# Input norm on per-token values, first input units in memory of their own, and a final stage in column halves, in a fused hybrid layer

## The chip, the cores and the metric

One core of a Trainium2 chip runs the whole program as one launch. The metric is the device time in microseconds of that core. All arrays are float32; matrix products are made of a high and a low part of each operand (fp32r), in three products each.

## What is computed

One inference step with one layer, for 512 latent tokens and 128 context tokens (640 in all), D = 2048:

```python
sh1, sc1, g1, sh2, sc2, g2 = split(silu(cond) @ w_ada + b_ada)      # for latent and for context tokens
h = rmsnorm(x, n1g) * (1 + sc1) + sh1
glu_in, q, k, v, ga, gb = split(h @ w_in)
conv_out = conformer_conv(glu_in)            # width 31, LayerNorm, swish, pointwise to 2048
attn_out = attention(rope(q), rope(k), v, cached k, cached v, sink)
x = x + g1 * ((sigmoid(ga) * conv_out + sigmoid(gb) * attn_out) @ w_out)
h2 = rmsnorm(x, n2g) * (1 + sc2) + sh2
gate, idx = top_k(softmax(h2 @ w_router).T, capacity)                # 16 experts: 64 latent, 16 context slots each
x = x + g2 * scatter_add(idx, gate * ((silu(h2[idx] @ w_g) * (h2[idx] @ w_u)) @ w_d))
y = rmsnorm(x, final_g)                      # outputs: y for both groups, k and v of the context
```

## The kernel before, in words

Each engine has a program of its own, written in order; they meet at semaphores. Weights come in units of 128 x 2048 values (1 MB), loaded by SyncE's queue in exactly the order of their use. Until the experts begin, the units go through a ring of four slots, `raw` (`raw_use` gives slot and count of use, L74). A slot is given back by `raw_freed`, two per use.

**Start.** SyncE's queue (`sync_program`, L328) loads `cond`, `x` in four parts (1.25 MB each), two units of `w_ada`, then units 0 and 1 of `w_in` into slots 2 and 3, then 30 more units of `w_ada`, each behind its slot. ScalarE squares the 16 channel tiles of `x` (L926) and VectorE adds them up (L1265). TensorE spreads the mean over all partitions with a matrix of 1/D (`mean_over_channels`, L625). VectorE adds EPS and takes the reciprocal (L1268, L1269), ScalarE the root (L939), VectorE makes one Newton step (L1271 to L1274), all on 128 x 640 values, and then the low halves of the two input units (`split_lo`, L1237); their high halves are ScalarE's (`split_hi`, L908).

A pair of ada units (shift and scale of one channel tile) is used by `ada_unit` (L589), 16 small matmuls of two passes per unit. The row is copied out (L915), folded (L597) and gets its bias (L1256). Then VectorE modulates the tile of `x` (L1280 to L1287), ScalarE and VectorE make its high and low half (L931, L1290), and TensorE uses it at once for both input units (`first_units`, L640; matmuls L610 to L612). So the first two dense units are made tile by tile beside the stream of ada units. When they end, ScalarE copies v of unit 0 out of PSUM (L962), makes the high half of unit 2, and TensorE goes on with unit 2 when both halves are there (`dense_start`, L617).

**Middle.** Dense units 2 to 39, then 32 gate units with attention, the convolution and two ada units to each, then attention out, conv out and `w_out` (16 units, 192 to 207 in the ring). In the last stage tokens and their modulated form go to DRAM (`tokens_acc`, `tokens_z`).

**Experts.** The expert weights are 24 units per expert through a ring of twelve (`ering`), which lies over the activations and raw slots 0 and 1. Unit j is loaded to slot (j + 10) % 12: units 0 and 1 go to the two raw slots when these are free, unit 2 when the last dense unit is done, and from unit 12 on each waits for the low half of the unit twelve before it (`ex_lo`, L371). After the routing (top-k on VectorE) POOL gathers the 80 token rows of expert 0 with an indirect DMA (L546) and gathers each next expert's rows beside the current one. TensorE needs the gathered rows to start. ScalarE casts a unit to its high half (L1160), VectorE subtracts for the low half (L1668), TensorE multiplies (L875). An expert's output columns 0 to 1023 are complete at unit 19, columns 1024 to 2047 at unit 23 (`slots_y`, L1689); POOL adds them to `tokens_acc` with one indirect DMA (`scatter`, L550).

**Tail.** When the last scatter has landed, SyncE's queue loads five tiles of 128 tokens (L381, 1 MB each). ScalarE squares each with its sum (L1197), VectorE and ScalarE make 1/rms for all five at once (L1738 to L1744, root L1200). Per tile VectorE scales (L1755), TensorE transposes in four groups (L899), ScalarE (L1205) and VectorE (L1749) multiply two groups each with the norm's weights, and SyncE's queue writes two outputs of 512 KB (L386). VectorE's order in that loop is: scale tile q, then its two groups of tile q - 1.

## Time and profile before

| | us |
|---|---|
| median of 3 runs | 3214.08 (3208.89 to 3214.21) |
| the profiled execution | 3212.56 |
| its span in the profile | 3210.8 |

The span is the time from the first to the last record of that one execution; the 1.8 us around it belong to the run. In the profile "busy" is time in which an engine executes, "idle before" what stood ahead of an instruction and what released it, and PEclk the share of its full clock that TensorE was granted (1.00 or 0.50). PEld is the loading of weights into TensorE, which lies beside matmuls. A DMA issue is named by the engine whose queue it stands in (SPq, POOL); its landing is when its semaphore is reached. "Issue" in the chain is time in which an engine waited for nothing that the profile shows.

### The profile page before, as it was taken

The numbers are of one execution on the slowest core, as the hardware profiler recorded it, in microseconds if no ns is written. First come the engines' busy times: TensorE is split into PE (matmuls) and PEld (weight loads), VectorE is DVE, ScalarE is ACT, GpSimd is POOL, SyncE is SP. The second block draws the span as 40 slices with busy tenths as digits, with TensorE's granted clock in tenths as the row PEclk, the third lists the DMA queues.
The fourth block names the chain that finished last, engine by engine and source line by source line (L and its number), as shares of the span: only waits on it lengthen the run. The fifth ranks groups of instructions, "written<-read, shape, count | busy, mean of one in ns | idle before, by whom it ended". The sixth has DMA issues, their size and how long they took to land.

```text
span 3210.8 us, 51984 instructions
## 1 busy us (share of the span) xinstructions
PE 3036.2 (95%) x20428; PEld 2579.3 (80%) x20428; DVE 1942.0 (60%) x2023; ACT 1349.6 (42%) x1479; POOL 275.8 (9%) x433
## 2 busy tenths in 40 slices
PE   5899999999999999989999999599999999999995
PEld 4899999989898998989999999366666666666663
DVE  6333322246565656665234333799999999998894
ACT  3211111133332333323112111477777777777774
POOL 0011110001111110110011111000000000000000
PEclk9999999999999999999999999799999999999997
DMA  9633332234444444453335432899999999999994
GB/s 367 266 128 119 119 127 78 78 112 171 171 168 180 165 167 173 174 211 114 128 148 187 130 128 85 309 364 398 382 379 369 389 387 389 384 378 374 382 376 139
DMA packets 124009, 746.06 MB, mean 232 GB/s; under 512 B 16720, under 2 KB 27008, under 8 KB 44080
## 3 DMA queue, kind: packets, MB, share of 16 engines
q1 hardware_dynamic: 97088, 636.54, 51.3%
q0 software_dynamic: 26768, 107.34, 10.8%
q8 instruction: 113, 1.85, 0.2%
q14 instruction: 40, 0.33, 0.0%
HBM read 681.60 MB, written 55.66 MB: 230 GB/s over the span
## 4 chain that ended last, share of the span: by engine, by line
PE 77%; DVE 9%; DMA 5%; issue 5%; ACT 3%; SPq 0%; DVEq 0%; POOL 0%; ACTq 0%; POOLq 0%
PE pu L875 22%; PE pu L610 15%; PE pu L611 15%; PE pu L612 15%; DVE elo L1668 4%; PE pt L589 2%; PE pt L721 2%; DMA raw<-in_w_ada 2%; ACT ehi L1160 2%; DVE xe L1680 1%; PE ps L691 1%; DVE wlo L1237 1%; PE ps L699 1%; PE pt L709 1%; DMA raw<-in_w_in 1%
## 5 line engine op out<-in xcount | busy, mean ns | idle before, releaser
L610 PE MATMUL pu<-hhi,whi 128*128 128x320 f32 x3328 | 1049.9, 315 | 19.9 <-DVE hlo L1446 11.0
L611 PE MATMUL pu<-hlo,whi 128*128 128x320 f32 x3328 | 1032.4, 310 | 0.0
L612 PE MATMUL pu<-hhi,wlo 128*128 128x320 f32 x3328 | 1032.3, 310 | 0.0
L1668 DVE TENSOR_TENSOR elo<-ering,ehi 128x2048 fp32r<-128x2048 f32 x384 | 874.8, 2288 | 107.0 <-ACT ehi L1160 103.3
L1160 ACT CAST ehi<-ering 128x2048 fp32r<-128x2048 f32 x384 | 731.4, 1912 | 238.2 <-PE pu L875 238.0
L610 PEld LDWEIGHTS pu<-hhi,whi 128*128 128x128 f32 x3328 | 629.3, 189 | 26.7 <-issue 17.5
L611 PEld LDWEIGHTS pu<-hlo,whi 128*128 128x128 f32 x3328 | 629.3, 189 | 1.9
L612 PEld LDWEIGHTS pu<-hhi,wlo 128*128 128x128 f32 x3328 | 628.6, 189 | 0.0
L908 ACT CAST whi<-raw 128x2048 fp32r<-128x2048 f32 x112 | 213.0, 1902 | 486.4 <-PE pu L612 463.0
L1237 DVE TENSOR_TENSOR wlo<-raw,whi 128x2048 fp32r<-128x2048 f32 x112 | 256.6, 2291 | 256.6 <-ACT whi L908 255.9
L875 PE MATMUL pu<-ehi,xhi 128*80 128x512 f32 x1024 | 322.0, 395 | 2.2
L875 PE MATMUL pu<-ehi,xlo 128*80 128x512 f32 x1024 | 320.4, 394 | 0.0
L875 PE MATMUL pu<-elo,xhi 128*80 128x512 f32 x1024 | 320.0, 393 | 0.0
L1408 DVE SCALAR_TENSOR_TENSOR ctmp<-zt,taps,ctmp 128x670 f32<-128x670 f32 x232 | 212.5, 916 | 28.3 <-DVE ctmp L1408 19.2
L875 PEld LDWEIGHTS pu<-ehi,xhi 128*80 128x80 f32 x1024 | 149.3, 148 | 89.8 <-DVE elo L1668 9.3
L875 PEld LDWEIGHTS pu<-elo,xhi 128*80 128x80 f32 x1024 | 151.6, 148 | 85.5 <-issue 0.7
L875 PEld LDWEIGHTS pu<-ehi,xlo 128*80 128x80 f32 x1024 | 151.5, 148 | 85.5 <-issue 0.7
L875 PE MATMUL pu<-ehi,hthi 128*80 128x512 f32 x512 | 162.8, 399 | 0.0
L875 PE MATMUL pu<-ehi,htlo 128*80 128x512 f32 x512 | 159.8, 393 | 0.0
L875 PE MATMUL pu<-elo,hthi 128*80 128x512 f32 x512 | 159.8, 393 | 0.0
L589 PE MATMUL pt<-raw,condw 128*32 128x128 f32 x3072 | 108.6, 286 | 16.8 <-DMA raw<-in_w_ada 16.7
L1023 ACT COPY pt_sb<-pt 128x512 f32<-128x512 f32 (+1 forms) x80 | 41.8, 523 | 183.3 <-PE pt L709 112.6
(252 smaller groups left out, 2619.3 us busy)
## 6 DMA issues: line engine op xcount, KB each, us to landing
ering<-in_w_experts SPq DMA_DIRECT2D x384, 1024.0 KB, 7.8
raw<-in_w_ada SPq DMA_DIRECT2D x96, 1024.0 KB, 7.0
raw<-in_w_in SPq DMA_DIRECT2D x72, 1024.0 KB, 4.8
raw<-in_w_attn_out SPq DMA_DIRECT2D x16, 1024.0 KB, 6.3
raw<-in_w_out SPq DMA_DIRECT2D x16, 1024.0 KB, 4.8
gates_tanh<-th POOLq DMA_DIRECT2D x32, 320.0 KB, 2.4
gl<-gates_tanh POOLq DMA_DIRECT2D x32, 320.0 KB, 3.5
raw<-in_w_conv_out SPq DMA_DIRECT2D x8, 1024.0 KB, 4.8
```

Source lines behind the costliest of these rows:

```text
L589: last = nc.tensor.matmul(bank[g:g + 32, 0:128], condw[:, kt, 30 - 2 * u:62 - 2 * u], raw[:, slot, kt * 128:kt * 128 + 128], start=u == 0 ...
L610: nc.tensor.matmul(o, whi[:, dk, w:w + 128], hi[:, kt, cols], start=kt == 0, stop=False)
L611: nc.tensor.matmul(o, whi[:, dk, w:w + 128], lo[:, kt, cols], start=False, stop=False)
L612: last = nc.tensor.matmul(o, wlo[:, dk, w:w + 128], hi[:, kt, cols], start=False, stop=kt == kts - 1)
L721: last = nc.tensor.matmul(pt[:, 0, 0:128], vg[:, v, :], pt_sb[:, 128 * b:128 * b + 128], start=b == 0, stop=b == len(vs) - 1)
L875: last = nc.tensor.matmul(pu[0:SLOTS, 2 * (h % 2) + c, :], left, ring[:, j % AHEAD, w:w + 512], start=k == 0 and left is hi and ring is eh ...
L908: nc.scalar.copy(whi[:, dk, :], raw[:, slot, :]).then_inc(hi_ready, 1)
L1023: last = nc.scalar.copy(pt_sb[:, 0:min(w, 512)], pt[:, 0, 0:min(w, 512)])
L1160: nc.scalar.copy(ehi[:, j % AHEAD, :], ering[:, slot, :]).then_inc(ex_hi, 1)
L1237: nc.vector.tensor_tensor(wlo[:, dk, :], raw[:, slot, :], whi[:, dk, :].bitcast(F32), ALU.subtract).then_inc(lo_ready, 1)
L1408: nc.vector.scalar_tensor_tensor(out=dst, in0=ztf[:, ds(zb, CO)], scalar=w, in1=ctmp[:, :], op0=ALU.mult, op1=ALU.add).then_inc(conv_done, 1)
L1668: nc.vector.tensor_tensor(elo[:, j % AHEAD, :], ering[:, slot, :], ehi[:, j % AHEAD, :].bitcast(F32), ALU.subtract).then_inc(ex_lo, 1)
```

## The change

Six things, with the code below:

- Input units 0 and 1 are loaded to `wfirst`, which lies over the end of `hlo`, ahead of all ada units, and the first four ada units are loaded without a wait. Every later position in the ring is two lower (`G_Q = A1 - 2`).
- The sums of squares are turned to one value per token and partition (five matmuls with one column each); the root and Newton step are made on 128 x 5 values; a product with the identity and a second `mean_over_channels` spread the result, which carries the factor D, over all partitions. TensorE does that after the first ada unit. The low half of unit 0 is made before the spread result is read, that of unit 1 after.
- Unit 1 of the first two dense units is made four channel tiles behind unit 0 (`LAG`), and its last five tiles follow the last of unit 0. ScalarE makes the high half of unit 2 before it copies v of unit 0.
- The load of expert unit 12 waits for the first gather.
- The last expert's scatter is two, one for each half of the columns. The tail's loads and squares are in halves too; the sums of both are added. Tile 0 has its 1/rms by itself, tiles 1 to 4 together (`FIN`). A root of one value ahead of the squares loads the table early.
- `rope_a`, `pool_passed` and `vec_passed`, on which nothing waits, are one semaphore. The hunks of that are left out below.

```diff
-G_Q = A1
+G_Q = A1 - 2
+LAG = 4
...
-    return raw_use(j if j < 2 else j + 2, 0, 1, 0, 0)
+    return raw_use(j, 0, 1, 0, 0)
...
+    wfirst, o = at("wfirst", [128, 2, UNIT], F32, R0 - 2 * UNIT * 4)
...
+        for d in range(2):
+            sp.dma_start(wfirst[:, d, :], a["w_in"][d]).then_inc(first_loaded[d], 16)
         for j in range(A1):
-            load(a["w_ada"][ada_of(j)], *ada_use(j), first=j < 2)
-            if j == 1:
-                for d in range(2):
-                    load(a["w_in"][d], 2 + d, 0, first=True)
+            load(a["w_ada"][ada_of(j)], *ada_use(j), first=j < RAW)
...
             if j < ERING - LEAD:
-                sp.wait_ge(raw_freed[j], 2 * (G_E // RAW))
+                sp.wait_ge(raw_freed[j], 2 * ((G_E + RAW - 1 - j) // RAW))
...
+            if j == ERING:
+                sp.wait_ge(xe_loaded, 16)
...
-        sp.wait_ge(ex_lo, NE * EU)
-        sp.wait_ge(y_added, 16 * NE)
-        for q in range(5):
-            sp.dma_start(fin[:, q, :], acc_d[128 * q:128 * q + 128, :]).then_inc(unit_loaded[q], 16)
+        sp.wait_ge(ex_lo, NE * EU - 5)
+        for h in range(2):
+            sp.wait_ge(y_last[h], 16)
+            cols = slice(1024 * h, 1024 * h + 1024)
+            for q in range(5):
+                sp.dma_start(fin[:, q, cols], acc_d[128 * q:128 * q + 128, cols]).then_inc(unit_loaded[5 * h + q], 16)
...
-            pool.wait_ge(y_made, 2 * e + 4)
-            scatter(e)
+            if e + 1 < NE:
+                pool.wait_ge(y_made, 2 * e + 4)
+                scatter(e)
+        for h in range(2):
+            pool.wait_ge(y_made, 2 * NE + 1 + h)
+            pool.indirect_dma_start(acc_d[:, :], bass.IndirectOffsetOnAxis(ap=idx_all[:, NE - 1:NE], axis=0),
+                                    ysl[:, 1024 * h:1024 * h + 1024], None, element_offset=1024 * h,
+                                    compute_op=ALU.add).then_inc(y_last[h], 16)
...
-        mean_over_channels(t1, ps, HALF, norm_mm)
+        for q in range(5):
+            last = nc.tensor.matmul(ps[:, 0, q:q + 1], t1[:, 128 * q:128 * q + 128], ones[:, 0:1], start=q == 0,
+                                    stop=True, skip_group_check=True)
+        last.then_inc(norm_mm, 1)
...
         def first_units(kt):
...
+            first_unit(0, kt)
+            if kt >= LAG:
+                first_unit(1, kt - LAG)
...
+            if j == 0:
+                pe.wait_ge(norm_t, 3)
+                mean_over_channels(t2, ps, HALF, norm_mm)
...
+        for kt in range(KT - LAG, KT):
+            first_unit(1, kt)
...
+        first_hi(0)
+        act.wait_ge(norm_t, 2)
+        nc.scalar.activation(nrm[:, 2, 0:5], nrm[:, 1, 0:5], ACT.Sqrt).then_inc(norm_sq, 1)
+        first_hi(1)
...
         for d in range(2 * NKV):
+            if d == 0:
+                split_hi(*raw_use(G_Q, 1, U, 0, 2), 2, 0)
             if d < NKV:
...
-            split_hi(*raw_use(G_Q, 1, U, 0, d + 2), d + 2, d % 2)
+            if d:
+                split_hi(*raw_use(G_Q, 1, U, 0, d + 2), d + 2, d % 2)
...
+        nc.scalar.activation(fst[:, 4, 7:8], ones[:, 0:1], ACT.Sqrt)
+        for h in range(2):
+            for q in range(5):
+                act.wait_ge(unit_loaded[5 * h + q], 32 * NE + 16)
+                if 5 * h + q >= 2:
+                    act.wait_ge(fin_sq, 5 * h + q - 1)
+                nc.scalar.activation(fsq[:, (5 * h + q) % 2, :], fin[:, q, 1024 * h:1024 * h + 1024], ACT.Square,
+                                     accum_out=fst[:, h, q:q + 1]).then_inc(fin_sq, 1)
+                if h == 1 and q == 2:
+                    tile_root(0)
+        tile_root(1)
...
+        mean, inv, root, fix = (nrm[:, k, 0:5] for k in range(4))
+        link(nc.vector.tensor_scalar(mean, ps[:, 0, 0:5], EPS, None, ALU.add))
+        nc.vector.reciprocal(inv, mean).then_inc(norm_t, 1)
         vec.wait_ge(norm_sq, 1)
...
+        link(nc.vector.tensor_tensor(fix, root, root, ALU.mult))
+        link(nc.vector.tensor_tensor(fix, fix, mean, ALU.mult))
+        link(nc.vector.tensor_scalar(fix, fix, -0.5, 1.5, ALU.mult, ALU.add))
+        link(nc.vector.scalar_tensor_tensor(out=root, in0=root, scalar=float(D), in1=fix, op0=ALU.mult, op1=ALU.mult))
+        t5 = [128, 5, 128]
+        nc.vector.tensor_tensor(t2[:, :].rearrange("p (q n) -> p q n", q=5), ident[:, :].unsqueeze(1).to_broadcast(t5),
+                                root.unsqueeze(2).to_broadcast(t5), ALU.mult).then_inc(norm_t, 1)
...
+        first_lo(0)
+        vec.wait_ge(norm_mm, 2)
+        link(nc.vector.tensor_copy(rstd[:, :].rearrange(c2, c=2), ps[:, :, 0:HALF]))
+        first_lo(1)
...
+        def tile_rstd(g):
+            q0, q1 = FIN[g]
+            s0, s1, root, ms, inv = (fst[:, n, q0:q1] for n in range(5))
+            vec.wait_ge(fin_sq, 5 + q1)
+            fc_link(nc.vector.tensor_tensor(ms, s0, s1, ALU.add))
+            fc_link(nc.vector.tensor_scalar(ms, ms, 1.0 / D, EPS, ALU.mult, ALU.add))
+            fc_link(nc.vector.reciprocal(inv, ms))
+            vec.wait_ge(fin_root, g + 1)
...
         for q in range(5):
+            if q < 2:
+                tile_rstd(q)
```

## Rows read from the trace of the kernel before

**Rows 1.** the page: the chain that ended last, by engine
```profile
PE 77%; DVE 9%; DMA 5%; issue 5%; ACT 3%; SPq 0%; DVEq 0%; POOL 0%; ACTq 0%; POOLq 0%
```

**Rows 2.** stretches: us; PE, PEld, DVE, ACT, POOL busy; PEclk, DMA, GB/s
```profile
3.00:26.30 23.30, 3.47 (x25) 2.17 (x28) 14.85 (x20) 12.91 (x18) 2.94 (x5) 1.00 0.99 407
26.30:38.70 12.40, 6.96 (x116) 5.22 (x106) 11.12 (x7) 6.24 (x6) 0.00 (x0) 0.74 0.55 189
60.00:100.00 40.00, 34.89 (x624) 29.46 (x624) 21.70 (x50) 7.14 (x16) 0.00 (x0) 1.00 1.01 420
124.50:127.90 3.40, 3.40 (x14) 3.40 (x14) 0.70 (x1) 2.56 (x3) 1.07 (x2) 0.50 0.88 364
```

**Rows 3.** timeline: start us, us, engine, line, instruction, idle before
```profile
22.83 2.47 PE L625 MATMUL ps<-t,ones 128*128 128x320 f32 x4 [22.83 <-DVE t L1265]
...
29.28 1.28 ACT L939 ACT_TABLE_LOAD   x1
...
34.45 2.29 DVE L1237 TENSOR_TENSOR wlo<-raw,whi 128x2048 fp32r<-128x2048 f32 x1
...
41.57 1.94 PE L589 MATMUL pt<-raw,condw 128*32 128x128 f32 x32 [4.06 <-DMA raw<-in_w_ada]
...
43.44 0.59 PE L597 MATMUL pt<-fold,row 128*128 128x4 f32 x2
```

**Rows 4.** the chain that ended last, start of the kernel: start us, us, what
```profile
101.34 8.73 DMA raw<-in_w_ada
...
124.65 0.27 PE pu L610
```

**Rows 5.** timeline of TensorE where the first two input units end
```profile
116.75 0.38 PE L610 MATMUL pu<-hhi,whi 128*128 128x320 f32 x1 [1.58 <-DVE hlo L1290]
...
118.64 0.76 PE L670 MATMUL pt<-ident,vst 128*128 128x128 f32 x5
123.09 0.39 PE L610 MATMUL pu<-hhi,whi 128*128 128x320 f32 x1 [3.68 <-issue]
```

**Rows 6.** first two gathers: POOL's timeline; then DMA views (2037, 2042 to 2043, 2052)
```profile
2037.78 2.55 POOL L546 DMA_INDIRECT xe<-tokens_z,idx_all  x1 [23.95 <-DVE idx_all L1659]
2052.47 0.94 POOL L546 DMA_INDIRECT xe<-tokens_z,idx_all  x1 [12.14 <-PE ps L846]
...
xe<-tokens_z,idx_all POOLq DMA_INDIRECT x1, 9.8
...
q1 hardware_dynamic: 54, 0.44, 104.3%
...
xe<-tokens_z,idx_all POOLq DMA_INDIRECT x1, 5.8
```

**Rows 7.** the chain that ended last, tail
```profile
3160.50 6.58 DMA tokens_acc<-ysl,idx_all
...
3185.73 0.18 DVE fst L1742
...
3186.34 1.30 DVE fin L1755
```

**Rows 8.** timelines of VectorE, ScalarE and SyncE's queue in the tail
```profile
3152.07 1.21 DVE L1695 TENSOR_TENSOR ysl<-pu,g2slot 80x1024 f32<-80x1024 f32 x1
...
3171.97 1.91 ACT L1197 ACTIVATE fout<-fin 128x2048 f32<-128x2048 f32 x1 [19.36 <-DMA fin<-tokens_acc]
...
3181.91 1.91 ACT L1197 ACTIVATE fout<-fin 128x2048 f32<-128x2048 f32 x1 [0.50 <-DMA fin<-tokens_acc]
...
3189.69 0.69 DVE L1749 TENSOR_TENSOR fout<-pu,norms 128x512 f32<-128x512 f32 x1 [0.86 <-PE pu L899]
...
3190.41 15.19 SPq L386 DMA_DIRECT2D out_y<-fout  x10
```

**Rows 9.** the scatter's line, all 16; a stretch of the outputs
```profile
DMA to landing us min/median/max: 6.6/7.0/12.1
...
3204.00:3206.00 2.00, 0.00 (x0) 0.00 (x0) 0.00 (x0) 0.00 (x0) 0.00 (x0) 0.50 0.99 282
```

More of the change, by code:

```diff
@@ L141, in build @@
     rstd, o = at("rstd", [128, N], F32, o)
+    nrm, _ = at("nrm", [128, 4, 8], F32, o - 2 * N * 4)
     assert o <= C0
@@ L262, in build @@
     cond_loaded = sem("cond_loaded")
+    first_loaded = [sem("first_loaded0"), sem("first_loaded1")]
     const_made, fold_made = sem("const_made"), sem("fold_made")
@@ L393, in settle @@
         def settle():
-            pool.sem_inc(pool_passed, 1)
+            pool.sem_inc(passed, 1)
         pool.memset(ident[:, :], 0.0).then_inc(const_made, 1)
@@ L637, in tensor_program, with first_unit @@
         pe.wait_ge(sq_summed, KT)
-        mean_over_channels(t1, ps, HALF, norm_mm)
-        def first_units(kt):
-            for d in range(2):
-                if kt == 0:
-                    dense_start(d, d)
-                pe.wait_ge(h_hi, kt + 1)
-                pe.wait_ge(h_lo, kt + 1)
-                dense(d, d, d, d, hhi, hlo, kt, kt + 1, 0, KT)
+        for q in range(5):
+            last = nc.tensor.matmul(ps[:, 0, q:q + 1], t1[:, 128 * q:128 * q + 128], ones[:, 0:1], start=q == 0,
+                                    stop=True, skip_group_check=True)
+        last.then_inc(norm_mm, 1)
+        def first_unit(d, kt):
+            if kt == 0:
+                dense_start(d, d)
+            pe.wait_ge(h_hi, kt + 1)
+            pe.wait_ge(h_lo, kt + 1)
+            dense(d, d, d, d, hhi, hlo, kt, kt + 1, 0, KT)
+        def first_units(kt):
+            first_unit(0, kt)
+            if kt >= LAG:
+                first_unit(1, kt - LAG)
         rows = (row0, row1)
@@ L926, in scalar_program, with first_hi @@
             nc.scalar.activation((t2 if kt % 2 else t3)[:, :], xin[:, kt, :], ACT.Square).then_inc(sq_made, 1)
+        def first_hi(d):
+            act.wait_ge(first_loaded[d], 16)
+            nc.scalar.copy(whi[:, d, :], wfirst[:, d, :]).then_inc(hi_ready, 1)
+        first_hi(0)
+        act.wait_ge(norm_t, 2)
+        nc.scalar.activation(nrm[:, 2, 0:5], nrm[:, 1, 0:5], ACT.Sqrt).then_inc(norm_sq, 1)
+        first_hi(1)
         act.wait_ge(small_loaded, 16 * 5)
@@ L936, in scalar_program @@
                 ada_read_out(*ada_use(j), pt[:, j // 2 % 2, :], rows[j // 2 % 2][:, :])
-            if j == 2:
-                act.wait_ge(norm_t, 2)
-                nc.scalar.activation(rstd[:, :], t2[:, :], ACT.Sqrt).then_inc(norm_sq, 1)
-                for d in range(2):
-                    split_hi(2 + d, 0, d, d)
             if j >= 3 and j % 2:
@@ L1189, in expert, with tile_root @@
                     turned_hi(xhi[:, 4 * g:4 * g + 4, :], TURNS * e + (6 + g), g % 2)
+        def tile_root(g):
+            act.wait_ge(fin_c, 7 * g + 3)
+            q0, q1 = FIN[g]
+            nc.scalar.activation(fst[:, 2, q0:q1], fst[:, 4, q0:q1], ACT.Sqrt).then_inc(fin_root, 1)
         with act.Fori(0, NE - 1) as e:
@@ L1193, in scalar_program @@
         expert(NE - 1, False)
-        for q in range(5):
-            act.wait_ge(unit_loaded[q], 32 * NE + 16)
-            nc.scalar.activation(fout[:, q, :, :].rearrange("p k c -> p (k c)"), fin[:, q, :], ACT.Square,
-                                 accum_out=fst[:, 0, q:q + 1]).then_inc(fin_sq, 1)
-        act.wait_ge(fin_c, 2)
-        nc.scalar.activation(fst[:, 2, 0:5], fst[:, 1, 0:5], ACT.Sqrt).then_inc(fin_root, 1)
+        nc.scalar.activation(fst[:, 4, 7:8], ones[:, 0:1], ACT.Sqrt)
[9 more added lines that the diff above has]
+        tile_root(1)
         for q in range(5):
@@ L1365, in maxima @@
                 vec.wait_ge(att_v, v + 1)
-                vec.sem_inc(vec_passed, 1)
+                vec.sem_inc(passed, 1)
                 m0 = 128 if j == 0 else 0
@@ L1734, in fc_link @@
             vec.wait_ge(fin_c, fc[0])
-        ss, inv, root, ms = (fst[:, n, 0:5] for n in range(4))
-        vec.wait_ge(fin_sq, 5)
-        fc_link(nc.vector.tensor_scalar(ms, ss, 1.0 / D, EPS, ALU.mult, ALU.add))
-        fc_link(nc.vector.reciprocal(inv, ms))
-        vec.wait_ge(fin_root, 1)
-        fc_link(nc.vector.tensor_tensor(inv, root, root, ALU.mult))
-        fc_link(nc.vector.tensor_tensor(inv, inv, ms, ALU.mult))
-        fc_link(nc.vector.tensor_scalar(inv, inv, -0.5, 1.5, ALU.mult, ALU.add))
-        fc_link(nc.vector.tensor_tensor(root, root, inv, ALU.mult))
+        def tile_rstd(g):
+            q0, q1 = FIN[g]
+            s0, s1, root, ms, inv = (fst[:, n, q0:q1] for n in range(5))
[4 more added lines that the diff above has]
+            vec.wait_ge(fin_root, g + 1)
+            fc_link(nc.vector.tensor_tensor(inv, root, root, ALU.mult))
+            fc_link(nc.vector.tensor_tensor(inv, inv, ms, ALU.mult))
+            fc_link(nc.vector.tensor_scalar(inv, inv, -0.5, 1.5, ALU.mult, ALU.add))
+            fc_link(nc.vector.tensor_tensor(root, root, inv, ALU.mult))
         def channels_out(q):
```

22 lines of the change are left out of this document (10 added, 12 removed).

## The prediction

> **What bounds the kernel now.** I read the page's chain first [rows 1]: 77% of it is TensorE, so time comes back only where TensorE stands still or is slowed. The change touches three such places, and I read a timeline and a table of stretches for each.
>
> The first is the start. The DMA engines move 407 GB/s from 3.0 to 26.3 us, only 189 from 26.3 to 38.7, and 420 afterwards [rows 2]. The timeline shows why [rows 3]: after x, two ada units and two input units all four raw slots are full. Slots 0 and 1 come free when TensorE, which starts at 22.83, has used the ada units; slots 2 and 3 only when VectorE has made the low halves of the input units, from 34.45 on, behind the norm chain on 128x640 values that begins when L625 ends at 25.3. From then on the ada units are a stream at the DMA's pace; the last is issued at 101.34 and landed 8.7 us later [rows 4]. What follows is work: the last tiles of units 0 and 1 start at 116.75, and unit 2 starts at 123.09, after a wait of 3.68 us for its halves [rows 5]. Then TensorE is granted 0.50 of its clock for 3.4 us, the lower of its two levels [rows 2].
>
> The second is the first gather: it is issued at 2037.78 and TensorE is idle until it has landed 9.8 us later [rows 6]. The third is the tail [rows 7, 8]: a scatter issued at 3160.50 takes 6.58 us, then come five loads of 1 MB whose squares start at 3171.97 and, for the last, 3181.91, a root, the scaling, and the first output at 3190.41. From there packets of 512 B keep the DMA full at 282 GB/s almost to the end [rows 9].
>
> **Part 1, the start.** *The slots.* Input units 0 and 1 go to memory of their own, so four ada units are queued without a wait, 2 x 1.05 MB more than before. The hole is (420 - 189) GB/s x 12.4 us = 2.86 MB, or 6.8 us at 420 GB/s. The queue that ran dry at 26.3 now lasts 5.0 us longer, to 31.3, and slot 0 must be free before that. VectorE's squares end at 22.8 as before. The five one-column products have no row; twice five weight changes lie between ten of the small matmuls (0.06 each, 32 in 1.94 [rows 3]) and L625's 2.47. I take 2.0, as the weights are as large as L625's: 24.8. The first ada unit costs 1.94, so slot 0 is free at 26.7, over 4 us before the queue is empty. TensorE then waits for the short chain: six operations on five columns at 0.2 a step [rows 7], a root of 0.25 (such an operation and its wait), and one 128x640 product with the identity, 0.8 (the share of 640 in the 2.29 for 2048, and a start): ready near 27.1. The root's table load of 1.28 [rows 3] starts once ScalarE has copied half 0, near 23.6, and is done before its input is. The second mean costs 2.47 and ends at 29.6; ada 1 follows and frees slot 1 by 31.6, while load 4 keeps the DMA busy to 33.8. Slots 2 and 3 follow at the stream's pace or faster, so I leave no hole: **-6.8**. Bounds: -3.4 if half of it stays (TensorE's new wait stands ahead of slots 1 to 3), -7.5 if the ramp after 38.7 goes too. Behind the same wait VectorE makes both low halves (2.29 each) and starts the first tile near 33, six us earlier than before, so it isn't late for the stream.
>
> *The lag.* In [rows 5] twelve matmuls take 1.89, 0.1 of it the start: 0.15 each, a tile of one unit 0.9. From the last low half of the activations: unit 0's last tile 0.9, then five tiles of unit 1, 4.5, then the transposes, 0.76 at most: 6.1 to unit 2. Its halves (1.91 on ScalarE, now ahead of v's copy, and 2.3 on VectorE) are done at 0.9 + 4.3 = 5.2, beside it. Before it was 123.09 - 116.75 = 6.3: **-0.2**. The tiles put off lie in time that TensorE had to spare beside the DMA (87% busy from 60 to 100 [rows 2]). The wait of 3.68 ahead of the fall of the clock is gone. In the slow stretch a matmul steps 0.27 instead of 0.15 [rows 4], so 3.4 us of it lose 1.5: **-1.5**, bounds 0 (another fall near by) and -1.7. v's copy comes 1.9 later, behind the split; POOL's stores behind it have unit 2's 14 us as cover.
>
> *Moved with it.* Every ring position is two lower. Expert units 0 and 1 wait for the splits of w_out units 14 and 15 instead of 12 and 13, two dense units of 96 matmuls, over 14 us each, later. On SP's queue unit 2 stands behind them, and that waits for the last dense unit anyway, which is over 20 us later still. I cost it at nothing; without that cover the first casts would be late by one load, some 5 us. The merged semaphores cost nothing.
>
> Sum of part 1: **-8.5**.
>
> **Part 2, the gather.** Unit 12 is issued as soon as unit 0's low half is made. From 2042 to 2043 all packets are the weight queue's, and the gather's come after them [rows 6]. The second gather, with nothing beside it, lands 5.8 after its issue; its issue instruction took 0.94 where the first one's took 2.55. Alone the first should need 5.8 + 1.6 = 7.4 instead of 9.8: **-2.4**. Bounds: 0 (the late start is the gather's own) and -4.0 (all that it is over 5.8). Behind SP's new wait stand units 12 to 14. The ring holds twelve units, and ScalarE's copies alone take nine times 1.91, 17 us, before unit 12 is wanted: nothing; without the ring, up to 7 us once.
> The Trainium skill (DMA: Bandwidth & Descriptors, "Queues, rings and completion order") says that each DMA engine takes turns between its rings, packet by packet. By that the gather would only have shared the engines, and holding the unit would give its 0.66 MB at 420 GB/s, 1.6 us instead of 2.4. The trace shows no such turn between 2042 and 2043.
>
> **Part 3, the tail.** Columns 0 to 1023 are ready at 3153.3 [rows 8]. Their scatter lands under the last 6 us of matmuls, by 3160; five loads of half a tile, 6.2 us of DMA, lie under the second scatter. That is issued at 3160.5 as before. Alone it took 6.58; the median of all 16, most of them beside the load stream, is 7.0 [rows 9]. I take 7.0: landed at 3167.5. Bounds 6.0 (half the bytes) and 12.1, the slowest of them. A load of 1 MB was there 4.8 after the scatter, 2.5 of it data (four more took 9.94), so a half is there after 3.6: 3171.1, and one more each 1.24. A square of 1024 columns is half of 1.91 and a little, 1.1, and its sum 0.1. Tile 2's ends at 3173.7 + 1.2 = 3174.9. Tile 0's root follows, 3175.1, then four operations, 0.8, and the scaling, 1.30: 3177.2. Meanwhile tiles 3 and 4 arrive, the last square ends at 3177.5. VectorE has the second chain and tile 1's scaling ahead of tile 0's output: 0.6 + 0.25 + 0.8 + 1.3 + 0.69 = 3.6, so the first output goes out at 3181.1, where it was 3190.41: **-9.3**. TensorE's transposes and ScalarE's share lie beside that. From the first issue to the end the outputs are bound by the DMA, 20.4 us as before. Bounds: loads of 4 KB rows at the 282 GB/s of the 512 B rows cost 3, a scatter at its slowest 5, and a scatter of 6.0 gains 1, a quicker start of the loads 0.7: -1.3 to -11.
>
> **Sum.** -8.5 - 2.4 - 9.3 = -20.2 against the profiled execution's 3212.56 (the span of 3210.8 and 1.8 around it): 3192.4, so **3192**. The three runs have their median at 3214.08, 1.5 above that execution, and go from 3208.89 to 3214.21, so 0.2% (6.4 us) is about what a measurement of this kernel can tell from no change.
>
> **Rivals.**
> *A. The hole stays by half and the second scatter is slow* (3200). TensorE's new wait ahead of ada 1 holds slots 1 to 3, and the loads of the first columns, queued in front of the second scatter, delay it. For it: scatters of up to 12.1 occur beside loads. Against it: load 4 alone bridges to 33.8. 3192 + 3.4 + 5 = 3200.
> *B. Root and square need different tables* (3196). In the tail the root's table is loaded ahead of the squares. If it holds no square, three loads of 1.28 stand in the chain, before tile 0's root, before tile 3's square and before the second root: 3192 + 3.8. For it: no row here has a square right behind a root. Against it: squares follow the swish's table with no load between.
> The Trainium skill (ScalarE: Activation LUTs, "Table sets: the hidden batching unit") says that cheap functions are in every set, but its list doesn't name the square; no row of this trace decides it.
> *C. Slower: TensorE stays at the low level during the ada stream* (3225). Place: the first four pairs of ada units have one dense tile instead of two, so TensorE is busy for some 70% where it was 87%. Price: at 0.50 an ada unit takes 1.94, the fold 0.59 [rows 3], a matmul 0.27: a pair with two tiles 7.7, with one 6.1. Ten of the one and four of the other from 31 on end at 132. With 15 more to unit 2 that is 147 in place of 123: +24, less 11.7 of parts 2 and 3, +12. It decides only if the level stays low although TensorE, then slower than the DMA, is busy all the time.
> *D. The change doesn't reach its aim* (3208). The hole only moves, the late start is the gather's own, and the tail gives what its first chain loses: about -5. Against it: each of the three waits has a named cause in the trace.
>
> **How the numbers follow.** Forecast 0.70 (3186 to 3197), A 0.12, B 0.10, C 0.03, D 0.05. All terms at their good ends give -7.5 - 1.9 - 4.0 - 11 = -24.4, 3188; the spread of the runs takes that to 3185. The upper end takes in A and B and the same spread, 3203; C, D and the forecast's edges are outside. Faster by over 0.2% is the forecast, A and B, 0.92; within 0.2% is D, 0.05; slower is C, 0.03.
>
> **What would show it.** Start: the DMA at 400 GB/s or more from 26 to 39, the last ada unit landed near 103, unit 2 started near 116, nothing at 0.50 in the 10 us behind it. Gather: landed 7.4 after its issue, no packet of a unit beside it. Tail: the second scatter landed near 3156.6 (3167.5 less the 10.9 of parts 1 and 2), the first output 20.6 us after that scatter's issue, 20 from there to the end. I would be wrong if there is a hole after 31 us, TensorE at 0.50 between 35 and 60, a table load among the last squares, or 25 us between the second scatter's issue and the first output.

## The result, and the profile after

The changed kernel takes 3193.18 us (median of 4 runs, 3192.81 to 3195.81) where the kernel before, beside it, took 3212.69 (3208.89 to 3214.21). The ratio is 0.9942, its 95% interval 0.9930 to 0.9954: faster by 19.5 us. The forecast was 3192. The two profiled executions are compared below; they lie 16.6 us apart in their spans (3210.8 and 3194.2), since the one after is the slowest of its four.

The chain that ended last, by engine, from the page of the kernel after, answers to [rows 1]; TensorE holds 78% of it, where it was 77%.

```profile
PE 78%; DVE 9%; DMA 5%; issue 4%; ACT 3%; POOL 0%; DVEq 0%; SPq 0%; ACTq 0%; POOLq 0%
```

The stretches of [rows 2] in the kernel after, with one more (54.4 to 57.8). Columns: us; busy time of PE, PEld, DVE, ACT, POOL; granted clock; DMA share; GB/s.

```profile
3.00:26.30 23.30, 3.34 (x34) 3.28 (x38) 14.62 (x22) 16.60 (x22) 2.95 (x5) 1.00 0.99 407
26.30:38.70 12.40, 9.51 (x156) 6.81 (x152) 10.88 (x18) 2.63 (x4) 0.00 (x0) 1.00 1.00 405
54.40:57.80 3.40, 3.40 (x38) 2.85 (x38) 0.47 (x1) 0.89 (x2) 0.00 (x0) 0.53 1.01 424
60.00:100.00 40.00, 34.92 (x634) 29.50 (x628) 22.14 (x50) 7.24 (x16) 0.00 (x0) 1.00 1.01 419
124.50:127.90 3.40, 3.40 (x25) 3.40 (x25) 0.00 (x0) 0.00 (x0) 0.00 (x0) 1.00 0.73 299
```

The hole of 189 GB/s is filled, to 405. The stretch at the low clock behind unit 2 is gone, but one stands in the modulation stream instead. It cost nothing there: the DMA ran at 424 GB/s through it, and TensorE waits for the DMA in this stage.

How the start got there: the timeline of TensorE and VectorE in the kernel after (start, duration, engine, line, instruction, idle time before). It answers to [rows 3].

```profile
22.96 2.26 PE L654 MATMUL ps<-ones,t 128*128 128x1 f32 x10 [22.96 <-DVE t L1310]
23.59 1.28 ACT L962 ACT_TABLE_LOAD   x1
25.15 1.93 PE L604 MATMUL pt<-raw,condw 128*32 128x128 f32 x32
25.25 0.17 DVE L1314 TENSOR_SCALAR nrm<-ps 128x5 f32<-128x5 f32 x1 [2.44 <-PE ps L654]
...
26.73 0.83 DVE L1322 TENSOR_TENSOR t<-ident,nrm 128x640 f32<-128x640 f32 x1
...
27.61 2.50 PE L640 MATMUL ps<-t,ones 128*128 128x320 f32 x4 [0.53 <-DVE t L1322]
30.04 3.64 PE L604 MATMUL pt<-raw,condw 128*32 128x128 f32 x64
...
33.30 0.82 DVE L1338 TENSOR_TENSOR xin<-xin,rstd 128x640 f32<-128x640 f32 x1
```

The one-column products took 2.26, the short chain was ready at 27.56 and the ada units behind it went through at 30.04. The end of this stage, from the chain that ended last (start, duration, what), with the transposes ahead of unit 2; it answers to [rows 4, 5]:

```profile
95.41 8.74 DMA raw<-in_w_ada
...
104.18 1.12 PE pt L604 x32
...
116.32 0.55 PE pt L697 x5
```

The last ada unit landed at 104.15 where it was 110.07, the last tiles started at 110.81 (116.75 before), and unit 2 follows the transposes directly at 116.9 (123.09 before). The first gather is next: POOL's timeline, VectorE's first use of the rows, and the issue view, as in [rows 6].

```profile
2028.85 0.17 DVE L1717 CAST idx_all<-pt 80x16 uint32<-80x16 f32 x1
...
2029.94 2.55 POOL L554 DMA_INDIRECT xe<-tokens_z,idx_all  x1 [23.95 <-DVE idx_all L1717]
...
2037.39 2.73 DVE L1738 SCALAR_TENSOR_TENSOR xe<-xe,shslot 80x512 f32<-80x512 f32 x4 [3.56 <-DMA xe<-tokens_z,idx_all]
...
xe<-tokens_z,idx_all POOLq DMA_INDIRECT x1, 7.4
```

Its issue was 7.84 us earlier than before (2037.78), its landing 2.4 us sooner after the issue (7.4 for 9.8). The tail, from the chain that ended last, answers to [rows 7]:

```profile
3142.30 3.22 POOL tokens_acc L579
...
3149.23 9.83 DMA tokens_acc<-ysl,idx_all
3159.07 0.32 SPq L389
...
3160.86 8.20 DMA fin<-tokens_acc
3169.08 1.16 ACT fsq L1241 x2
...
3172.00 1.29 DVE fin L1818
```

The second scatter, which forecast and code put on the path, took 9.83 us, not 7.0. SyncE's queue shows the early loads and the outputs (start, duration, queue, line, instruction); its second row answers to the output row of [rows 8]:

```profile
3149.07 12.36 SPq L389 DMA_DIRECT2D fin<-tokens_acc  x10
3173.91 14.98 SPq L394 DMA_DIRECT2D out_y<-fout  x10
```

| Part | forecast | profiled executions |
|---|---|---|
| last ada unit landed (the slots) | -6.8 | -5.9 |
| last tiles to unit 2 (the lag) | -0.2 | -0.3 |
| unit 2 to the first gather (the clock) | -1.5 | -1.6 |
| gather, issue to landing | -2.4 | -2.4 |
| sixteen experts, first rows to last output value | 0 | -1.1 |
| last output value to the end | -9.3 | -5.3 |
| sum | -20.2 | -16.6 |

The last row is the miss: from the last ysl (3159.00 before, 3147.73 after) to the end of the span it was 51.8 us and is 46.5. The others come to within 1 us of the forecast. The row of the experts is no part of the change: behind the first gather TensorE's low level ended 2.1 us sooner after the rows had landed (6.8 for 8.9 us), and the first twelve matmuls took 3.84 us for 4.80. The clock's row is only in part the clock of the start. At 131.6 us in the kernel after, its lead was 8.0 us, 6.2 of them from before unit 2, so the missing low stretch gave 1.8. From there to the gather the lead went between 4.4 and 9.3 us, and that it stood at 7.8 in the end is chance.

### The profile page after: what moved, and what is told of

It is laid out like the page before. It is cut to its first block, busy times and chain, and to the rows that moved or that the text cites. A ratio compares the mean times of both kernels' runs of the same rounds, so it can differ in the third digit from the quotient of the medians.

```text
span 3194.2 us, 52056 instructions
## 1 busy us (share of the span) xinstructions
PE 3037.8 (95%) x20438; PEld 2580.5 (81%) x20438; DVE 1938.1 (61%) x2033; ACT 1350.6 (42%) x1491; POOL 279.1 (9%) x434
## 3 DMA queue, kind: packets, MB, share of 16 engines
q0 software_dynamic: 26864, 107.34, 10.9%
## 4 chain that ended last, share of the span: by engine, by line
PE 78%; DVE 9%; DMA 5%; issue 4%; ACT 3%; POOL 0%; DVEq 0%; SPq 0%; ACTq 0%; POOLq 0%
PE pu L902 24%; PE pu L625 15%; PE pu L626 15%; PE pu L627 15%; DVE elo L1726 4%; PE pt L604 2%; PE pt L748 2%; DMA raw<-in_w_ada 2%; ACT ehi L1195 2%; DVE xe L1738 1%; PE pt L736 1%; PE ps L726 1%; PE ps L718 1%; DMA raw<-in_w_in 1%; DVE wlo L1282 1%
## 5 line engine op out<-in xcount | busy, mean ns | idle before, releaser
L1466 DVE SCALAR_TENSOR_TENSOR ctmp<-zt,taps,ctmp 128x670 f32<-128x670 f32 x232 | 212.6, 917 | 28.3 <-DVE ctmp L1466 19.2
```

The lines of the kernel that those rows point to most:

```text
L1466: nc.vector.scalar_tensor_tensor(out=dst, in0=ztf[:, ds(zb, CO)], scalar=w, in1=ctmp[:, :], op0=ALU.mult, op1=ALU.add).then_inc(conv_done, 1)
```

## The experiments

Two theories stood at first. The forecast's: each of the three waits has its own cause, and the tail fell short because loads that are issued ahead of a scatter hold it back. The rival: the DMA engines share, the scatter is slow beside anything, and lag and hold are worth nothing by themselves.

### The norm on 128x640 again, the input units still in memory of their own

```diff
-        for q in range(5):
-            last = nc.tensor.matmul(ps[:, 0, q:q + 1], t1[:, 128 * q:128 * q + 128], ones[:, 0:1], start=q == 0,
-                                    stop=True, skip_group_check=True)
-        last.then_inc(norm_mm, 1)
+        mean_over_channels(t1, ps, HALF, norm_mm)
```
(and the chain of root and correction on 128x640 values, as before the change, without the second mean)

> The changed kernel with the norm on 128x640 values as before (one spread mean, no wait of TensorE behind the first ada unit); memory of its own for input units 0 and 1 and the lag stay. Theory 'both are needed': the four ada units bridge the old hole at 26 to 38.7 us, but VectorE comes to the first tile at 39 as before, ada unit 4 waits for the bias of tile 0, slots stay full and the DMA has a hole of about 2 us near 41 to 44; last ada unit landed near 106, against 104.1 in the changed kernel. Rival 'the memory alone does it': no hole, landed at 104.1. Rival 'the norm does it': a hole of over 5 us, landed at 109 or more.

One run, 3198.87 us where the kernel before took 3209.98 beside it. Its stretches:

```profile
26.30:38.70 12.40, 4.88 (x118) 3.38 (x110) 11.43 (x7) 2.95 (x4) 0.00 (x0) 0.82 1.01 421
38.70:45.00 6.30, 4.96 (x70) 4.11 (x71) 4.81 (x13) 1.29 (x3) 0.00 (x0) 0.54 0.71 270
```

The hole of before is filled here too, but a new one opens behind it: 270 GB/s from 38.7 to 45.0, while TensorE stands at 0.54 of its clock. The last ada unit landed at 106.5, between 110.1 (before) and 104.1 (after). So by this run own memory alone brings 3.6 of the 5.9 us, the short norm the other 2.3; the new hole is 1.8 us of DMA time (0.29 of 6.3 us). TensorE's low level isn't the cause of the hole by itself: in a version further below, with the increment and no lag but the short norm, TensorE stood at 0.55 from 38.7 to 45.0 too, and the DMA went on at 416 GB/s. But that execution also had its last ada unit only at 106.6, as its DMA moved 376 GB/s from 45 to 60 at a share of 0.98. A landing in one execution is therefore good to some 2 us, and the split of 3.6 and 2.3 is an indication.

### No lag of the second unit

```diff
-LAG = 4
+LAG = 0
```

> The changed kernel with LAG = 0: both units at every tile. If the lag is what keeps TensorE busy at the end of units 0 and 1, a wait of about 3.7 us comes back ahead of unit 2 (less 0.9, since unit 2's high half is still made ahead of v's copy: 2.8), and the clock falls to 0.50 for 3.4 us within 10 us of it, as before. If the low stretch at 54.4 to 57.8 us of the changed kernel comes from its lighter first pairs, it is gone here. Rival: the low stretches fall where they like, one stays near 55 and none follows unit 2's start. Last ada unit landed at 104.1 either way.

One run, 3194.32 us, which is within what the changed kernel does. The wait of 2.8 us came back as expected, 1.97 us ahead of the transposes and 0.80 behind them, but the clock stayed at 1.00 from 112 to 132. And unit 2 started at 116.7, 5.5 us after the last tiles; with the lag it is 6.1, since five tiles of unit 1 lie there. So up to this point the lag costs 0.5 us, and what gains on the 6.3 us of before is that ScalarE makes unit 2's high half ahead of v's copy. By this run alone the lag is worth nothing. I come back to it below: one run misled.

### No hold ahead of the 13th expert unit

```diff
-            if j == ERING:
-                sp.wait_ge(xe_loaded, 16)
```

> The changed kernel without the wait for the first gather ahead of expert unit 12. Theory 'in order': a gather issued behind a unit's load starts when that load's packets are through; landed 9.8 us after its issue instead of 7.4, no packet of it in the first 2.5 us behind its issue. Rival 'taking turns': 9.0 us (0.66 MB more at 420 GB/s), packets of both side by side from the start. Rival 'its own latency': 7.4.

One run, 3202.42 us. Its time can't be read as the price of the hold: its routing ended at 2032.93, 4.1 us later than in the profile after, before the missing wait can act. What can be read is the stretch from issue to landing: 9.6 us. The issue view around 2033, and the packets of both queues from 2040 to 2042:

```profile
xe<-tokens_z,idx_all POOLq DMA_INDIRECT x1, 9.6
...
q0 software_dynamic: 67, 0.55, 105.9%
q1 hardware_dynamic: 5, 0.00, 0.1%
```

From 2036 to 2040 the weight queue q1 moved 0.28 and 0.77 MB, one unit of 1.05 MB, and the gather's queue q0 only 0.09. Then q0 had the engines to itself. The gather stood behind the whole unit. It wasn't late by itself: with the hold its first packet came 3.2 us after its issue, here 5.8, and the unit's packets began 2.7 us after that issue. Had the queues taken turns, the gather would have moved as much as the weights from 2038 on. GpSimd's issue instruction had begun first (2034.02, the unit's load 2035.74), but it took 2.55 us, and the load came before its end. The Trainium skill (DMA: Bandwidth & Descriptors, "Queues, rings and completion order") says that an engine takes turns between rings packet by packet; these rows don't agree.

### The first column half waits for both scatters

```diff
-            sp.wait_ge(y_last[h], 16)
+            sp.wait_ge(y_last[0], 16)
+            sp.wait_ge(y_last[1], 16)
```

> The changed kernel with all ten half-tile loads of the tail behind both scatters. Theory 'in order' for the tail's miss: in the changed kernel the second scatter took 9.83 us because the first loads stood in the DMA queues ahead of it; with nothing ahead it lands 6.2 us after its issue (5.5 to 6.6). The first output then comes 6.2 + 3.6 + 9 x 1.24 + 1.2 + 3.6 = 25.8 us after that issue, against 24.7 in the changed kernel. Rival 'the scatter of half rows right behind another is slow by itself': it takes 9.8 again, and the first output comes after 29.4.

One run, 3196.73 us. The chain in its tail:

```profile
3148.19 4.96 DMA tokens_acc<-ysl,idx_all
...
3157.06 10.37 DMA fin<-tokens_acc
```

With no load ahead of it the second scatter takes 4.96 us, half of 9.83. The rival (a scatter is as slow as that by itself) is out. But the last load landed 19.2 us after the scatter's issue, where it was 19.8 in the kernel after. Halving the scatter and giving up the early loads came to nearly the same for the loads. The first output came at 26.6 us, 1.9 later than with early loads, since all ten squares now queue behind them.

### The tail's part alone

The kernel before, and in it of the change only the column halves, the two scatters, the early loads and the two groups of roots:

```diff
-        sp.wait_ge(ex_lo, NE * EU)
-        sp.wait_ge(y_added, 16 * NE)
-        for q in range(5):
-            sp.dma_start(fin[:, q, :], acc_d[128 * q:128 * q + 128, :]).then_inc(unit_loaded[q], 16)
+        sp.wait_ge(ex_lo, NE * EU - 5)
+        for h in range(2):
+            sp.wait_ge(y_last[h], 16)
+            cols = slice(1024 * h, 1024 * h + 1024)
+            for q in range(5):
+                sp.dma_start(fin[:, q, cols], acc_d[128 * q:128 * q + 128, cols]).then_inc(unit_loaded[5 * h + q], 16)
...
```

> The kernel before with the tail's part of the change alone (column halves, two scatters, early loads, roots in two groups), start and gather as before. Theory (parts add): from the last expert output value to the end 46.5 us in place of 51.8, the kernel 5 to 6 us faster than before, with the second scatter landing 9 to 10 us after its issue. Rival (the whole gain is one sum in which the parts disturb each other): 2 us or less faster, or the full 9 us of the forecast.

3206.91 us (median of 11 runs), the kernel before 3212.68 (15 runs): ratio 0.9984, interval 0.9975 to 0.9993. That is 5.8 us faster (interval 2.2 to 8.0), where the sum by parts has 5.3; the gain of the tail stands without the other parts, and neither 2 us nor 9 is likely. The profiled execution bears the size out less well: from the last ysl to the end it took 47.7 us (3156.15 to 3203.9), 4.1 less than before and not 5.3. Its second scatter took 8.94 us, but its last load landed 21.1 us after that scatter's issue, 1.3 later than in the kernel after; why, one execution doesn't show.

### The second scatter ahead of the loads, in two versions

```diff
+        sp.wait_ge(y_free, NE + 1)
         for h in range(2):
             sp.wait_ge(y_last[h], 16)
@@ GpSimd, behind the two half scatters
+        pool.sem_inc(y_free, 1)
```

> SyncE's five loads of the first column half wait until GpSimd has issued the second scatter. Theory (a scatter's packets begin only behind the transfers that were issued ahead of it on the other queue): the second scatter now lands 5 to 6.5 us after its issue, the last half-tile load lands about 2 to 4 us earlier than in the changed kernel as it stands (counted from the second scatter's issue: 16 to 18 us in place of 19.8), and the kernel is 2 to 4 us faster than the changed kernel. Rival (the queues share, and the ten half-tile loads are limited by their own sum of bytes behind whatever starts first): the scatter is faster, but the first-half loads start as much later, so that the last load lands no earlier and the time is within 1 us of the changed kernel's.

> The changed kernel once more, as the yardstick for the three runs beside it. Expected: a time 0.5 to 0.7% below the kernel before, that is 16 to 22 us, with the second scatter of the 13th expert landing 9 to 10 us after its issue and the last half-tile load landing some 20 us after that issue.

(The second is the changed kernel without an edit, run beside the first. Its text names the scatter of the 13th expert; it is the last expert's, the 16th.) The version with the increment took 3191.80 us (3190.61 to 3195.36) beside the changed kernel's 3195.57 (3190.78 to 3198.70). The two ratios to the kernel before are 0.9938 (0.9924 to 0.9951) and 0.9944 (0.9931 to 0.9958). The medians look like a gain, but the trace says that nothing was tried: the increment, written behind the scatter, took effect before the scatter's instruction ran. SyncE's loads were issued at 3144.03, 0.05 us ahead of the scatter, and the scatter took its time as before.

```profile
3144.03 12.30 SPq L390 DMA_DIRECT2D fin<-tokens_acc  x10
...
3144.08 9.91 DMA tokens_acc<-ysl,idx_all
```

In the next version an instruction that GpSimd itself executes, behind the scatter, gives the signal:

```diff
-        pool.sem_inc(y_free, 1)
+        pool.memset(fst[:, 3, 6:7], 0.0).then_inc(y_free, 1)
```

> SyncE's loads of the first column half wait for a small memset that GpSimd executes behind the second scatter, so that they are issued 1.4 to 1.6 us after its issue begins and not 0.04 us before it. Theory (transfers of the two queues go in the order in which they were handed over, scatters behind loads issued ahead of them): the second scatter lands 5 to 6.5 us after its issue, the last half-tile load lands 16 to 18 us after that issue in place of 19.8, and the kernel is 2 to 4 us faster than the changed kernel beside it. Rival (no order, the queues share 16 engines, and the scatter of 0.65 MB beside loads is slow in any case): the second scatter still takes 8 us or more, and the time stays within 1 us of the changed kernel's.

> The changed kernel as the yardstick of the two runs beside it: 0.5 to 0.7% below the kernel before, second scatter 9 to 10 us, last load 19.8 us after the second scatter's issue.

The version with the memset took 3190.73 us (3189.22 to 3194.98; ratio 0.9936, interval 0.9922 to 0.9949) beside 3193.15 (3190.40 to 3195.01; 0.9939, 0.9925 to 0.9952). By their times these can't be told apart, by their traces they can. Its queue and chain:

```profile
3145.62 6.78 SPq L390 DMA_DIRECT2D fin<-tokens_acc  x10
...
3144.03 5.12 DMA tokens_acc<-ysl,idx_all
...
3151.85 11.81 DMA fin<-tokens_acc
```

The scatter landed after 5.12 us: order is what counts, and 1.6 us of it are enough. Which instruction begins first isn't the order that counts: in four executions the loads were issued 0.08 to 0.17 us after the scatter's instruction had begun, but within the 1.4 us that it takes, and the scatter still took 8.7 to 9.8 us. Here they are issued when it has ended. But the last load landed at 3163.66, 19.6 us after the scatter's issue (20.0 in the kernel beside it). What the scatter gave, the loads took: 14.5 us from the scatter's landing to theirs, where it is 10.9 beside. The reason is in the stretches of this kernel (columns as above):

```profile
3146.00:3148.00 2.00, 0.00 (x0) 0.00 (x0) 0.00 (x0) 0.00 (x0) 0.00 (x0) 0.50 1.07 141
3148.00:3150.00 2.00, 0.00 (x0) 0.00 (x0) 0.00 (x0) 0.00 (x0) 0.00 (x0) 0.50 0.98 338
3150.00:3152.00 2.00, 0.00 (x0) 0.00 (x0) 0.00 (x0) 0.34 (x1) 0.00 (x0) 0.50 0.93 229
3152.00:3154.00 2.00, 0.00 (x0) 0.00 (x0) 0.00 (x0) 1.48 (x3) 0.00 (x0) 0.50 1.01 381
3154.00:3156.00 2.00, 0.00 (x0) 0.00 (x0) 0.00 (x0) 1.63 (x4) 0.00 (x0) 0.50 1.02 416
```

The DMA engines are full from 3146 on, first with the scatter, which fills them at 141 GB/s. All ten loads are 5.24 MB, 12.5 us at the 420 GB/s of [rows 2], and the scatter comes on top of them. As far as these executions show, from the moment when the first half may be read this sum sets the last load, whichever of the two goes first: over nine executions with the tail of the change as it stands the last load landed 19.3 to 20.0 us after the second scatter's issue, in the two with the memset 19.6 and 19.0. And in the first 4 us of the loads the engines are as good as full (0.98 and 0.93) at only 338 and 229 GB/s. The kernel before, whose loads have rows of twice the length, was at 410 two us after its start:

```profile
3168.00:3170.00 2.00, 0.00 (x0) 0.00 (x0) 0.00 (x0) 0.00 (x0) 0.00 (x0) 0.50 0.88 262
3170.00:3172.00 2.00, 0.00 (x0) 0.00 (x0) 0.00 (x0) 0.03 (x1) 0.00 (x0) 0.50 0.98 410
```

In the kernel after a slow start comes twice, once for each half, though there the share also falls, to 0.80 and 0.79:

```profile
3151.00:3153.00 2.00, 0.00 (x0) 0.00 (x0) 0.00 (x0) 0.54 (x1) 0.00 (x0) 0.50 1.03 272
3153.00:3155.00 2.00, 0.00 (x0) 0.00 (x0) 0.00 (x0) 0.61 (x2) 0.00 (x0) 0.50 0.80 188
...
3159.00:3161.00 2.00, 0.00 (x0) 0.00 (x0) 0.00 (x0) 1.75 (x5) 0.00 (x0) 0.50 0.99 375
3161.00:3163.00 2.00, 0.00 (x0) 0.00 (x0) 0.00 (x0) 1.47 (x3) 0.00 (x0) 0.50 0.91 270
3163.00:3165.00 2.00, 0.00 (x0) 0.00 (x0) 0.48 (x3) 0.70 (x2) 0.00 (x0) 0.50 0.79 250
3165.00:3167.00 2.00, 0.00 (x0) 0.00 (x0) 0.00 (x0) 1.57 (x3) 0.00 (x0) 0.50 1.00 401
```

Why half-tile loads start so slowly isn't shown. It isn't which half: where the second half was queued while the first still ran, its packets went at 416 from the start. With all ten issued in one go, in the kernel that waits for both scatters, they still began at 289 and 229. That stays open.

### The lag once more, timed

The same edit as above, once in the version with the increment, once in the changed kernel:

```diff
-LAG = 4
+LAG = 0
```

> As the run before, and the second projection unit no longer lags behind the first (lag 0 in place of 4). Theory (the lag hides a wait of 0.8 us at the end of the modulation stage, and where the clock's low stretches fall is not set by it): within 1.5 us of the run before, on either side. Rival (the lag keeps the clock up behind the modulation stage, as the forecast had it, 1.5 us): slower than the run before by 1.5 us or more, with a stretch at granted clock 0.50 around 120 us.

> The changed kernel with a lag of 0 in place of 4 tiles, timed. The median of the forecast's claim (the lag keeps TensorE's clock up behind the modulation stage, worth 1.5 us) is 1.5 us slower than the changed kernel beside it, with a stretch at granted clock 0.50 within 10 us behind the second unit's start (around 118 to 130 us). Rival (the lag is worth nothing and the stretches fall by themselves): within 1 us, no such stretch.

3196.49 us (3194.71 to 3197.82) beside 3191.80 for the same kernel with the lag; 3197.27 (3193.97 to 3198.53) beside 3193.15. The ten runs without the lag have a mean of 3196.45, the ten of the changed kernel beside them 3193.88; the difference of 2.6 us is good to 2 us either way (worked out from the spread of the twenty). Both profiles have what the first run lacked, a low clock where unit 2 starts. The stretch from each of the two, lag 0, in the order of the runs:

```profile
119.10:122.60 3.50, 3.50 (x16) 3.50 (x15) 0.00 (x0) 3.11 (x3) 1.07 (x2) 0.55 0.71 255
```
```profile
115.20:122.10 6.90, 6.36 (x25) 5.99 (x26) 2.85 (x2) 3.19 (x3) 1.62 (x3) 0.52 0.58 225
```

So in two of three executions without the lag the clock fell around unit 2's start, and in none of the nine profiled executions with it. The two profiled executions whose start is that of before (the kernel before and the tail's part alone) have it too. Counted along ScalarE's instructions, which are the same in number, these two fell back by 1.3 and 2.2 us between the last tiles (109.1 in the kernel after) and v's copy behind unit 2 (131.6); the one without a low stretch gained 0.3, and the eight others with the lag stayed as they were. Against that one the two low stretches cost 1.6 and 2.5 us, as the second is twice as long; the mean of the three is 1.1, with the lag's own cost taken off. So the lag is worth something, in the mean less than the forecast's 1.5, and not the nothing of the first run. Three executions are few, and in the first of the two 2.3 us were lost before 100 us already, which is no part of this.

What is left of the medians' difference, and most of the spread of every kernel here, arises later. The same instruction at 1200 us stood 3.9 us ahead of the profile after in one execution of the changed kernel and 0.1 in another, with no edit between them. Of the 3.9 us 1.4 arise between 848 and 856 us and 1.6 between 1034 and 1046; there TensorE is at 0.50 in the profile after, from 849.5 to 852.9 and from 1037.2 to 1040.6, and at 1.00 in the other. The index cast that ends the routing, in these two:

```profile
2023.78 0.17 DVE L1717 CAST idx_all<-pt 80x16 uint32<-80x16 f32 x1
```
```profile
2027.39 0.17 DVE L1717 CAST idx_all<-pt 80x16 uint32<-80x16 f32 x1
```

### The first tile out ahead of the second's scaling

```diff
-                if h == 1 and q == 2:
+                if h == 1 and q == 1:
                     tile_root(0)
@@ VectorE
             if q < 2:
                 tile_rstd(q)
+            if q == 1:
+                channels_out(0)
...
-            if q:
+            if q > 1:
                 channels_out(q - 1)
```

> The version with GpSimd's memset behind the second scatter, and in it VectorE copies the first tile's channels out before it scales the second tile (not after), and the first tile's root comes one square earlier on ScalarE. Theory (from the first output on, the end is set by the outputs' own bytes, 20.3 us, so that only the moment of the first output counts): counted from the second scatter's issue the first output is issued at 23.2 us in place of 24.5, and the span ends 1.2 us earlier; no gap opens in the output traffic, since scale, transposes and copies of a tile (some 3.1 us) fit into the 3.7 us of its bytes. With the 0.3 us of the version before, from the second scatter's issue to the end 43.5 us in place of the changed kernel's 45.2; the median 1 to 3 us below the changed kernel's. Rival (VectorE's chain of scales and copies sets the end): the first output comes earlier, but a gap opens behind the second tile and the end stays within 0.3 us.

The edit is made in the version with the memset. It took 3195.83 us (3189.76 to 3198.08; ratio 0.9939, interval 0.9926 to 0.9953). As a time this says nothing; in its profile the routing ended at 2032.59, late by itself. In the tail the first output came 22.6 us after the second scatter's issue (24.5 without this edit, 24.8 in the changed kernel beside them), and the end 43.8 us after it (44.8 and 45.2). Of the 1.9 us by which the first output is earlier, 0.7 are the loads' (the last landed 19.0 us after the scatter's issue and not 19.6) and only 1.2 the edit's. The half that is missing between 1.9 and 1.0 is a gap behind the first tile:

```profile
3180.00:3182.00 2.00, 2.00 (x16) 2.00 (x16) 1.12 (x2) 1.80 (x7) 0.00 (x0) 0.81 0.57 172
```

The outputs fall from 280 GB/s to 172 while TensorE, still at its low level, transposes the second tile: 3.69 us for its sixteen products, which take 2.13 for each of the last two. In the version without this edit TensorE had no wait of 2.1 us between the first two tiles, and the second took 2.20. Theory and rival are each half right.

## Why the prediction was right, and where it was off

**Part 1** stood as forecast. The five one-column products took 2.26 (2.0 taken), the short chain was ready 0.5 us later than forecast, the root's table load lay beside TensorE's work. Of the 0.9 us that are missing from the 6.8, the stretch that was the hole takes half, as it runs at 405 and not 420 GB/s (15 x 12.4 us are 0.19 MB, 0.44 us); the other half I can't place, the stream behind it has 415 to 425. The run with the wide norm shows that the short chain was needed besides the memory. The lag's -0.2 measured -0.3, but the lag itself costs 0.5 there, and ScalarE's new order gives 0.8. The clock's -1.5 measured -1.8 in the two profiles; without the lag a low stretch came in two of three executions and cost 1.6 and 2.5 us. That TensorE might be at its low level between 35 and 60 I had named as a sign of being wrong; it was, for 3.4 us, and as the DMA was full throughout (424 GB/s), rival C had its mechanism and no price.

**Part 2** was exact, 7.4 us. The run without the hold gave 9.6 and showed why: the gather waits for the unit that was handed over before its issue had ended.

**Part 3** had the wrong size, -5.3 for -9.3. The first output came 24.7 us after the second scatter's issue, where the sum had 20.6; I had named 25 as the sign of being wrong. The steps that failed are two: "I take 7.0" for the scatter (9.8, +2.8), and "one more each 1.24" for the second half's loads, together with 3.6 for the first of them (the last landed 10.0 us after the scatter, for 8.6, +1.4). The row for the scatter was the median of scatters beside a weight stream that is spaced out; here five loads were handed over just ahead of it, at 3149.07 against 3149.23. Rival A had this mechanism; its other half, the hole, didn't come. But the runs show that the two terms are one: in the two executions with the scatter at 5.1 and 5.2 the last load came 19.6 and 19.0 us after its issue, where it is 19.3 to 20.0 in the nine with early loads. The step behind both is "five loads of half a tile, 6.2 us of DMA, lie under the second scatter". They can't lie under it; the DMA share was 0.79 to 1.03 in every two us from 3151 to 3167, so what goes under the scatter is taken from it. The end from the first output on was forecast at 20.4 and took 20.3.

**Rival B** is out. Behind the one table load at 3141.36 no other stands among squares and roots, so the square is held by the root's table. The Trainium skill (ScalarE: Activation LUTs, "Table sets: the hidden batching unit") says that cheap functions are in every set; it doesn't name the square among them, and the trace shows it in this one. **Rival D** named the tail's loss as one of three; two of its three parts didn't occur.

So the total owes its closeness to parts 1 and 2 and to luck: by the profiled executions the sum was 3.6 us too large, it would have been 4.7 without the 1.1 of the experts, and that the median after lies 2.6 us below its profiled execution made up for most of the rest.

## What to carry to other kernels

Where an indirect transfer from GpSimd is on the path, look at what the other queue is handed before GpSimd's issue instruction has ended: here the gather waited for all of a unit handed over 0.8 us before that end, and the scatter took 9.8 us for 5.1 beside loads handed over at the same moment. A short hold of that queue was worth 2.4 us where the engines were empty otherwise (one unit); it was worth 1 us at most where the held transfers were needed at the same end. And an edit that should give or take 1 to 2 us is to be read by stretches within several profiled executions: one run without the lag gave the wrong answer, and two timed medians of the changed kernel without an edit differed by 2.4 us.

## What I had not expected

- GpSimd's issue of a scatter took 3.22 us for the first half and 1.40 for the second, with the same shape. The kernel before has one of the longer kind too, for its 15th expert (3.23 against 1.44).
- A semaphore increment written behind GpSimd's scatter came ahead of it: SyncE's loads were issued 0.05 us before the scatter's instruction began. With the increment on a memset that GpSimd executes behind the scatter they came 1.6 us after that begin.
- Loads of 128 rows of 4 KB began at 190 to 340 GB/s, at DMA shares of 0.79 to 1.03, for some 4 us each time, and reached 371 to 416 afterwards.
- Without any edit, the end of the routing moved by 5 us between executions (2023.78 to 2028.85 in three profiles of the changed kernel); where TensorE's low stretches fell on the way accounts for 3.0 of it in the two places looked at above.
